# A hybrid encoder trunk on one core: the mean copied between the last diagonals, one convolution tile placed and centred in one step, and the first loads cut into smaller pieces

## The reference, cut to what matters

```python
def mixer_conformer_conv(x, w_pw1, b_pw1, w_dw, b_dw, ln_g, ln_b, w_pw2):
    h = x @ w_pw1 + b_pw1
    a, g = jnp.split(h, 2, axis=-1)
    h = a * jax.nn.sigmoid(g)
    h = causal_depthwise_conv(h, w_dw) + b_dw      # 31 taps, one filter a channel
    h = jax.nn.silu(layer_norm(h, ln_g, ln_b))     # mean and variance over 1024 channels
    return h @ w_pw2
```

## Time and profile before

| | |
|---|---|
| median of 3 runs | 2630.68 us (2630.32 to 2630.86) |
| the profiled execution | 2630.04 us |
| its span, first to last instruction | 2628.3 us |
| outside the span | 1.74 us |
| TensorE busy | 2582.5 us, 98% |
| VectorE busy | 1416.4 us, 54% |
| ScalarE busy | 1068.0 us, 41% |
| mean granted TensorE clock | 0.996 of full speed |

### The profile page before, as it was taken

One profiled execution on the slowest core, in us unless ns is written; L12 is line 12 of the kernel. 1 busy time (PEld: TensorE's weight loads), 2 busy tenths in 40 slices (PEclk: granted clock), 3 DMA queues, 4 the chain that ended last, 5 costly groups with the idle time before them and its releaser, 6 DMA issues. The chain is left out here.

```text
span 2628.3 us, 34068 instructions
## 1 busy us (share of the span) xinstructions
PE 2582.5 (98%) x14609; PEld 2241.3 (85%) x14609; DVE 1416.4 (54%) x1634; ACT 1068.0 (41%) x1769; POOL 1.4 (0%) x10
## 2 busy tenths in 40 slices
PE   8989999999999999999999999999999989999999
PEld 7879888889888898888898898888898979888888
DVE  6967333267554663332774473332677967333276
ACT  6875322235333252222362243222356865222235
POOL 0000000000000000000000000000000000000000
PEclk9999999999999999999999999999999999999999
DMA  4202333323222223333233323333223103333322
GB/s 151 73 9 84 110 96 96 104 97 121 88 96 89 89 82 99 99 99 103 82 97 96 97 72 113 96 96 105 96 83 99 58 22 96 96 96 97 104 84 77
DMA packets 192730, 239.63 MB, mean 91 GB/s; under 512 B 14860, under 2 KB 138564, under 8 KB 192452
## 3 DMA queue, kind: packets, MB, share of 16 engines
q1 hardware_dynamic: 192580, 237.46, 28.3%
HBM read 233.21 MB, written 2.10 MB: 90 GB/s over the span
## 5 line engine op out<-in xcount | busy, mean ns | idle before, releaser
L1536 DVE TENSOR_TENSOR w_lo<-raw,w_hi 128x1024 fp32r<-128x1024 f32 x432 | 518.8, 1221 | 576.7 <-ACT w_hi L1137 575.8
L1137 ACT CAST w_hi<-raw 128x1024 fp32r<-128x1024 f32 x432 | 446.0, 1047 | 687.0 <-DMA raw<-in_ffn_w_up_dram 331.0
L763 PE MATMUL psum<-a_hi,w_lo 128*128 128x512 f32 x928 | 361.2, 389 | 0.0
L765 PE MATMUL psum<-a_hi,w_hi 128*128 128x512 f32 x928 | 361.0, 389 | 0.0
L764 PE MATMUL psum<-a_lo,w_hi 128*128 128x512 f32 x896 | 348.6, 389 | 0.0
L763 PE MATMUL psum<-h_hi,w_lo 128*128 128x512 f32 x872 | 341.3, 391 | 0.0
L765 PE MATMUL psum<-h_hi,w_hi 128*128 128x512 f32 x872 | 339.3, 389 | 0.0
L764 PE MATMUL psum<-h_lo,w_hi 128*128 128x512 f32 x856 | 333.1, 389 | 0.0
L901 PE MATMUL psum<-a_hi,w_lo 128*128 128x256 f32 x1088 | 280.2, 286 | 4.2 <-DVE w_lo L1536 2.7
L901 PE MATMUL psum<-a_hi,w_hi 128*128 128x256 f32 x1088 | 276.6, 283 | 0.0
L901 PEld LDWEIGHTS psum<-a_hi,w_lo 128*128 128x128 f32 x1088 | 208.6, 192 | 5.6 <-DVE w_lo L1536 3.3
(11 more groups left out here) (291 smaller groups left out, 4080.1 us busy)
## 6 DMA issues: line engine op xcount, KB each, us to landing
raw<-in_ffn_w_gate_dram SPq DMA_DIRECT2D x176, 256.0 KB, 2.8
raw<-in_ffn_w_up_dram SPq DMA_DIRECT2D x176, 256.0 KB, 3.1
raw<-in_ffn_w_down_dram SPq DMA_DIRECT2D x176, 256.0 KB, 2.8
raw<-in_a_w_pw_dram SPq DMA_DIRECT2D x96, 256.0 KB, 2.9
raw<-in_ple_w_gate_dram SPq DMA_DIRECT2D x64, 256.0 KB, 2.8
raw<-in_b_w_in_dram SPq DMA_DIRECT2D x64, 256.0 KB, 2.9
raw<-in_c_w_in_dram SPq DMA_DIRECT2D x48, 256.0 KB, 3.0
raw<-in_b_w_out_dram SPq DMA_DIRECT2D x32, 256.0 KB, 2.8
```

The source lines that it names most:

```text
L763: pe.matmul(bank(grp.g, j), st_lo, mv_hi, start=(k == 0), stop=False, skip_group_check=by_tiles(grp))
L765: done = pe.matmul(bank(grp.g, j), st_hi, mv_hi, start=False, stop=(ku == last and a == UK - 1), skip_group_check=by_tiles(grp))
L1137: act.copy(hi_u[u % RING], raw_u[u % RING]).then_inc(hi_ready, 1)
L1536: dve.tensor_tensor(lo_u[u % RING], raw_u[u % RING], hi_u[u % RING].bitcast(F32), ALU.subtract)\
```

## The change

- The mean is copied to on-chip memory (`save_centre`) between the parts of tile 7's diagonals, not behind all of them. `LAST_PARTS` has five parts where it had three, and the product with the matrix of ones comes after tap 1 instead of tap 6. Phase 3 is copied out right behind the mean, ahead of the diagonals of taps 14 to 26.
- Tile 6 (phase 3, the fourth phased tile) is no longer placed by ScalarE. VectorE adds its bias and subtracts the mean in one instruction (`place_centred`), from the turned copy. Tiles 4, 5 and 7 are centred in two instructions, and the sums on VectorE are in another order. The squares of tiles 0 to 3 go to another place.
- x is loaded in pieces of 128, 128, 256, 256 and 256 columns. The first weight unit is loaded in two halves of 128 rows (`load_first`, two DMAs each) from ScalarE's queue; ScalarE and VectorE split each half by itself, and TensorE waits for each half by itself.

```diff
--- before.py
+++ after.py
@@ -14,13 +14,13 @@
 SEQ = 512
 DEPTH = 4
 CHUNK = 64
-X_COLS = 256
+X_PIECES = ((0, 1), (1, 1), (2, 2), (4, 2), (6, 2))
 TAPS_A = 31
 TAPS_C = 3
 TAPS_PE = 27
-LAST_PARTS = ((0, 9), (9, 18), (18, TAPS_PE))
+LAST_PARTS = ((0, 9), (9, 14), (14, 18), (18, 22), (22, TAPS_PE))
 TAPS_LAST = 15
-CENTRE_AT = 6
+CENTRE_AT = 1
 K_SHARED = 12
 PHASED = ((4, 0), (5, 0), (3, K_SHARED), (6, 0))
 TILE_ROWS = P // 2
@@ -523,7 +523,10 @@
         mix_done = sem("mix_done")
         uf_ready = sem("uf_ready")
         sgu_landed = sem("sgu_landed")
-        x_landed = [sem(f"x_landed{c}") for c in range(D_MODEL // X_COLS)]
+        x_landed = [sem(f"x_landed{c}") for c in range(len(X_PIECES))]
...
@@ -612,9 +615,10 @@
 
             def load_x(c):
 
-                sp.dma_start(x_in.rearrange("p (t d) -> p t d", t=TT)[:, :, c * X_COLS:(c + 1) * X_COLS],
-                             ins["x"][0].rearrange("(t p) d -> p t d", p=P)[:, :, c * X_COLS:(c + 1) * X_COLS])\
-                  .then_inc(x_landed[c], 16)
+                m, n = X_PIECES[c]
+                columns = slice(m * P, (m + n) * P)
+                sp.dma_start(x_in.rearrange("p (t d) -> p t d", t=TT)[:, :, columns],
+                             ins["x"][0].rearrange("(t p) d -> p t d", p=P)[:, :, columns]).then_inc(x_landed[c], 16)
 
...
@@ -651,12 +655,17 @@
                             sp.dma_start(p_raw.rearrange("p (t d) -> p t d", t=TT),
                                          ins["p"][s.layer, 0].rearrange("(t p) d -> p t d", p=P))\
                               .then_inc(p_landed, 16)
-                        if grp.unit + ku < len(x_landed):
-                            load_x(grp.unit + ku)
+                        u = grp.unit + ku
+                        if u == 0:
+                            load_x(0)
+                            load_x(1)
+                            continue
+                        if u + 1 < len(x_landed):
+                            load_x(u + 1)
...
-                        load(grp.unit + ku, parts_of(s, grp, ku * UK))
+                        load(u, parts_of(s, grp, ku * UK))
...
@@ -698,7 +707,7 @@
 
             def turn_x(m):
 
-                pe.wait_ge(x_landed[m * P // X_COLS], 16)
+                pe.wait_ge(x_landed[next(c for c, (m0, n) in enumerate(X_PIECES) if m0 <= m < m0 + n)], 16)
...
@@ -738,6 +747,8 @@
                 slot, by_token = (grp.unit + ku) % RING, s.kind == "sgu_v"
                 first = grp.unit == 0
                 for a in range(UK):
+                    if first and ku == 0:
+                        pe.wait_ge((first_lo, lo_ready)[a], 1)
...
@@ -1083,7 +1094,8 @@
                     turn_mix(s)
                 take_half(grp.g)
                 for ku in range(grp.units):
-                    pe.wait_ge(*lo_of_unit(grp.unit + ku))
+                    if grp.unit + ku > 0:
+                        pe.wait_ge(*lo_of_unit(grp.unit + ku))
...
@@ -1129,6 +1141,16 @@
         @block.scalar
         def _(act):
             own = Steps(act, act_step)
+
+            def load_first(a, landed):
+
+                view, columns = w_src(stages[0])
+                dst = raw_u[0].rearrange("p (a n) -> p a n", a=UK)
+                for i, (c, _) in enumerate(columns):
+                    act.dma_start(dst[:, a, 256 * i:256 * (i + 1)], view[:, a, c:c + 256]).then_inc(landed, 16)
+
+            load_first(0, first_landed)
+            load_first(1, raw_landed[0])
             act.wait_ge(const_ready, 3)
 
...
@@ -1145,8 +1167,14 @@
                 split_end[0] = max(end, split_end[0])
 
             act.copy(ones_r[:, :], ones[:, :]).then_inc(prm_ready, 1)
+            act.wait_ge(first_landed, 32)
+            act.copy(hi_u[0][:, 0:BANK], raw_u[0][:, 0:BANK]).then_inc(first_hi, 1)
             for m in range(DT):
-                if m % UK == 0:
+                if m == 1:
+                    act.wait_ge(raw_landed[0], 32)
+                    act.copy(hi_u[0][:, BANK:2 * BANK], raw_u[0][:, BANK:2 * BANK]).then_inc(hi_ready, 1)
+                    split_end[0] = 1
+                if m and m % UK == 0:
                     split_to(m // UK + 1)
                 act.wait_ge(xf_ready, m + 1)
                 act.copy(tiles(h_hi, m), tiles(xf, m)).then_inc(x_hi_ready, 1)
@@ -1230,15 +1258,18 @@
                 act.activation(tiles(h_f32, CONV_Y + m), conv_x[:, m, k:k + SEQ], ACT.Identity,
                                bias=col("a_b_dw", c, m), scale=col("a_w_dw", c * TAPS_A + k, m)).then_inc(conv_begun, 1)
 
+            def save_centre(s):
+
+                act.wait_ge(centre_done, s.layer // 3 + 1)
+                act.activation(mean[:, :], bank(s.taps_g + 1, 0), ACT.Copy, scale=2.0).then_inc(centre_saved, 1)
+
             def conv_squares(s):
 
                 c = s.layer // 3
-                act.wait_ge(centre_done, c + 1)
-                act.activation(mean[:, :], bank(s.taps_g + 1, 0), ACT.Copy, scale=2.0).then_inc(centre_saved, 1)
                 act.wait_ge(z_ready, 6 * c + 1)
-                act.activation(tiles(tmp, 0, 4), tiles(h_f32, CONV_Y, 4), ACT.Square).then_inc(sq_ready, 1)
+                act.activation(tiles(h_f32, 0, 4), tiles(h_f32, CONV_Y, 4), ACT.Square).then_inc(sq_ready, 1)
                 act.wait_ge(z_ready, 6 * c + 4)
-                act.activation(tiles(h_f32, 0, TILES - 1), tiles(h_f32, CONV_Y + TILES, TILES - 1), ACT.Square)\
+                act.activation(tiles(h_f32, TILES, TILES - 1), tiles(h_f32, CONV_Y + TILES, TILES - 1), ACT.Square)\
                     .then_inc(sq_ready, 1)
 
             def conv_last_square(s, h):
@@ -1386,12 +1417,13 @@
                         phase_place(s, 0)
                         more_blocks(s, 3, phase_part(3), TAPS_A)
                         phase_evict(s, 2)
-                        for part in range(len(LAST_PARTS)):
+                        last_diags(s, 0)
+                        phase_place(s, 1)
+                        last_diags(s, 1)
+                        save_centre(s)
+                        phase_evict(s, 3)
+                        for part in range(2, len(LAST_PARTS)):
                             last_diags(s, part)
-                            if part == 0:
-                                phase_place(s, 1)
-                        phase_evict(s, 3)
-                        phase_place(s, 3)
                         conv_squares(s)
                         conv_norm(s)
...
@@ -1545,12 +1577,24 @@
             def lo_more(n=1):
                 lo_to(lo_end[0] + n)
 
+            def first_weight_lo(a, ready, done):
+
+                dve.wait_ge(ready, 1)
+                part = slice(a * BANK, (a + 1) * BANK)
+                dve.tensor_tensor(lo_u[0][:, part], raw_u[0][:, part], hi_u[0][:, part].bitcast(F32), ALU.subtract)\
+                   .then_inc(done, 1)
+
             for m in range(0, DT, UK):
                 for i in range(m, m + UK):
                     dve.wait_ge(x_t_done, i + 1)
                     dve.tensor_copy(tiles(xf, i), bank(1, i % TILES)).then_inc(xf_ready, 1)
+                    if i == 0:
+                        first_weight_lo(0, first_hi, first_lo)
+                        lo_end[0] = 1
                 lo_to(m // UK + 1)
                 for i in range(m, m + UK):
+                    if i == 1:
+                        first_weight_lo(1, hi_ready, lo_ready)
                     dve.wait_ge(xf_ready, i + 1)
                     lo_of(x_hi_ready, i + 1, tiles(h_lo, i), tiles(xf, i), tiles(h_hi, i))
...
@@ -1578,6 +1622,13 @@
                 own.settle()
                 y = by_phase(tiles(h_f32, CONV_Y + PHASED[n][0]))
                 own.add(dve.tensor_tensor(y, y, phased(turned(n)[1]), ALU.add))
+
+            def place_centred(s, n):
+
+                m = PHASED[n][0]
+                dve.wait_ge(phase_turned[n], 64 * (s.layer // 3 + 1))
+                dve.scalar_tensor_tensor(by_phase(tiles(h_f32, CONV_Y + m)), phased(turned(n)[1]), col("a_b_dw", s.layer // 3, m),
+                                         by_phase(mean[:, :]), ALU.add, ALU.subtract).then_inc(z_ready, 3)
 
             def conv_sums_of(s):
 
@@ -1587,25 +1638,28 @@
                 dve.wait_ge(centre_saved, c + 1)
                 dve.tensor_tensor(three(y(0, 4), 4), three(y(0, 4), 4), many(mean[:, :], 4), ALU.subtract).then_inc(z_ready, 1)
                 own.settle()
-                dve.wait_ge(phase_placed, (len(PHASED) - 1) * (c + 1))
-                dve.tensor_tensor(three(y(4, 4), 4), three(y(4, 4), 4), many(mean[:, :], 4), ALU.subtract).then_inc(z_ready, 3)
+                dve.wait_ge(phase_placed, 2 * (c + 1))
+                own.add(dve.tensor_tensor(three(y(4, 2), 2), three(y(4, 2), 2), many(mean[:, :], 2), ALU.subtract))
+                own.add(dve.tensor_tensor(y(7, 1), y(7, 1), mean[:, :], ALU.subtract))
                 dve.wait_ge(z_ready, 6 * c + 1)
                 own.add(dve.tensor_tensor(both, y(0, 2), y(2, 2), ALU.add))
```

(27 more changed lines are left out.)

## The result

The changed kernel takes 2608.97 us (median of four runs, 2608.67 to 2609.39), against 2630.5 us before (2630.14 to 2630.86): 21.5 us less, a ratio of 0.9918 with a 95% interval of 0.9901 to 0.9935. The forecast was 2608.5. The profiled execution took 2609.23 us with a span of 2607.4; for it the forecast had 2607.9, from 2630.04 before.

A forecast was written before the change was run, and what follows sets the result against it. The prediction took the stage as bound by the mean copy's place in ScalarE's queue. Gains of 9.35, 9.6 and 3.2 us sum to 22.15, from 2630.68 to 2608.5 us; range 2604.5 to 2617.

The forecast's parts named there:

- What bounds: Convolution stage: TensorE's 9.0 us stand, twice, is bound by where the mean copy stands in ScalarE's queue.
- ScalarE's order, rebuilt: Layer 0's stage: mean copy after tap 13, diagonals end at 154.9, 2.6 us later, a new TensorE stand of 1.45 us.
- VectorE: Layer 0's sums: no wait for phase 3's DMAs, `place_centred` 0.75 us, line 1617 starts at 161.83, 8.34 us earlier.
- What is late next: After the stage: the norm chain, not the taps, releases line 1293; gain 9.35 us in layer 0, 9.6 in layer 3.
- Line 813's stands of 0.7 us: TensorE's two waits, read as standing behind line 810's 9.0 us stands and gone with them.
- The start: First loads: first product at 7.1 instead of 10.32, ended by x's second piece; gain 3.2 us, ends 1.4 and 4.7.
- Rival A: First loads: the start gains nothing or 1 us because the DMA engines are full anyway; 2611.7 or 2610.7 us; chance 0.15.
- Rival B: Convolution stage: ScalarE's diagonals become the bound, costing 4 to 5 us a layer; 2618.1 us; chance 0.10.
- C: Convolution stage: mean copied early, but VectorE ends where it did; only the start's gain is left, 2627.5 us; chance 0.04.
- D: TensorE's queue, tap 1 of tile 7: late `ysum` makes it slower, 1 us a layer per microsecond of lateness; chance 0.03.
- The sign that the prediction gave: TensorE's granted clock in the window behind line 810's counterpart: 1.00, not 0.72.

The follow-up runs named there:

- stage_only: The changed convolution stage with the first loads as before, against the kernel before: 2611.0 us, ratio 0.9928.
- late_out: The changed kernel, but ScalarE copies phase 3 out behind all diagonals, the mean copy staying early: 2620.4 us, ratio 0.9962 to the kernel before.
- one_queue: The changed kernel, but SyncE issues both halves of the first weight unit, between the x pieces: 2609.4 us, ratio 0.9926 to the kernel before.
- fill: The changed kernel with two more taps of diagonals ahead of the mean copy: 2607.1 us, ratio 0.9913 to the kernel before.
- wide_x: The changed kernel with x in four pieces of 256 columns again: 2610.6 us, ratio 0.9930 to the kernel before.
- fill_twice: The same kernel as `fill`, run again on another chip: 2607.5 us, ratio 0.9915 to the kernel before.
- fill_old_start: `stage_only` with two more taps of diagonals ahead of the mean copy: 2609.7 us, ratio 0.9927 to the kernel before.

## Why the prediction was right, point by point

**What bounds.** Right, with one addition. `stage_only` has the stand gone, so it hung on ScalarE's order. But it hung on two things in it: with the mean copy early and only phase 3's copy-out late (`late_out`), 4.6 of the 9.0 us are back. The prediction named the mean copy alone as the bound, and had put the copy-out early in its own rebuilt order.

**ScalarE's order, rebuilt.** With the 3.04 us of the start added, the mean copy began at 146.25 (foreseen 146.25), the first squares at 154.84 (154.9), TensorE got the last part at 154.99 (155.05). The stand for the last part was 1.25 us (1.45).

**VectorE.** `place_centred` took 0.75 us, the value taken between 0.7 and 1.2. The DMAs did not hold it up. Line 1671 started at 161.75 (161.83).

**What is late next.** Right: the norm chain, no longer the taps. The stage gave 9.32 and 9.53 us (foreseen 9.35 and 9.6). One reading was wrong, though no term of the sum hung on it. Line 813's stands of 0.7 us were not behind the 9.0 us stand but at the sums of h = 1 (186.78 and, in layer 3, 2145.73), and the change does not remove them: layer 3's is still there, and layer 0's is missing only because of the slow stretch.

**The start.** The place of the gain was right, its size nearly, and what ends the wait was not: 2.67 us at the first product and 3.04 at the stage, 2.8 in time, for 3.2. The second x piece was there at 6.2 (6.0), and its transposes were done by 7.35. What ended the wait was a leg that I had put at 6.0 to 6.6: x's first piece came at 5.04, later than the larger one of before (4.45), so that tile 0 was rounded only at 7.5, and the product waited 0.31 us for it. Some of the agreement is luck, because the trace of before from which I took the cost was at the slow end: the old loads gave a first product at 10.32, 9.34 and 8.82 us in three traces, the new ones with small x pieces at 7.25 to 7.68 in nine. One profiled execution did not show that spread; the bounds of 1.4 to 4.7 covered it.

**Rival A** had the rule right and the consequence wrong, as `one_queue` shows. **Rival B** named the resource that did become the bound, at a cost of 1.2 us a layer and not 4 to 5, and `fill` takes that back. **C** and **D** did not come about: VectorE waited 1.05 us for the mean, and ScalarE's 1.46 us of waiting was for a product that TensorE issued at 142.77, 2.2 us behind the end of `ysum` (140.55).

**What no step had.** The stretch at half clock in layer 0, 1.36 us of which 0.85 come back, behind two stands of which the first follows from the forecast's own times and the second was there before. The sign that the prediction gave, a granted clock of 1.00 behind the stand, held from 160 to 163 us and failed from 168 on. The later weight unit behind layer 3's norm, 0.4 us.

**Luck in the number.** Against the profiled execution the forecast is 1.3 us off (2607.9 for 2609.23): the start was over-estimated and the two losses above were not foreseen. The median is only 0.5 us off, because the 0.64 us that I added to get from the profiled execution to the median came out as 0.26 the other way. The stage was well understood; the last microsecond was not.

## What to carry to other kernels

When an engine stands for a result, follow the chain back to the last instruction that could have run earlier, and ask what stands ahead of it in its own queue: here a 0.57 us copy and the copy-out of phase 3 stood behind 26 small activations that could wait, and together that cost 9 us twice. Moving the mean copy alone is a little under half; the transfer that the next consumer needs must leave early too. Small work that has no consumer yet (diagonals, a table load) belongs into the waits that remain. Of first loads, cut and order the pieces by what the first product needs, from whichever queue.

## What the runs showed of the hardware

The granted clock fell to half behind stands of 1.56 and 0.99 us in three of three traces of the changed kernel, always in layer 0 and never in layer 3, where the stands are the same. It fell in layer 3 and not in layer 0 when the same stage came 2.8 us later (`stage_only`), and in neither when it came 2.2 us later (`wide_x`, 1.00 in all windows from 162 to 174). The filled kernel itself did both: in layer 0 its clock was 0.79 and 0.64 in the windows 165 to 168 and 168 to 171 of `fill`, and 1.00 in both in `fill_twice`, where the stage came 0.7 us later behind the same stands (1.8 and 1.0 us). The stands alone don't decide, then; where they fall in time seems to as well. The Trainium skill ("TensorE: Matmul & The Clock Gate", Part 1: The HAM clock gate) says that the monitor behind the clock is free-running and does not start with the kernel, which is in keeping with this.

What such a drop costs depends on the stand behind it. In the 26 convolution stages of the 13 traces the clock fell between the norm's first matmul and the sums of h = 1 in 12, and in just these 12 TensorE's stand of 0.68 to 0.70 us at line 824 (by the numbers of the changed kernel) is missing. So a drop like that of the changed kernel costs 1.36 us where it happens and some 0.5 us in the end, and the longer one of `fill_old_start` cost 1.7 us. Comparisons of edits that shift a stage carry this much noise in each layer.

At the start of the changed kernel the matmuls of lines 764 and 765 followed one another every 0.43 us until 10.8 us, and the 512-wide ones after that every 0.23 us, while the granted clock reads 1.00 from the beginning. That column does not show the slow first microseconds.
